# One-core Trainium2 kernel: the order of the last expert rows, of the last gate chunk and of the final stores

## The chip, the cores and the metric

The kernel runs on one core of a Trainium2 chip. The metric is device time in microseconds (us) of one execution; three runs of the kernel before give the median. The profile is of one more execution, and its trace counts from the first instruction of the span.

## What is computed

One layer of a hybrid encoder, 256 tokens by 2048 columns in float32: token mixers, a product-key expert network, and a gated embedding. The change touches the end of it:

```python
def peer_ffn(...):      # 8 heads, 16 experts each, per token
    a = gelu(einsum('thkd,td->thk', expert_u[idx], xb))
    return einsum('thk,thkd->td', g * a, expert_v[idx])
...
h = h + peer_ffn(rmsnorm(h, norm_ffn), ...)
gate = sigmoid(rmsnorm(h, norm_ple) @ w_ple_gate)     # 2048 x 2048
h = h + gate * (p @ w_ple)
return rmsnorm(h, norm_final)
```

## The kernel before

Every engine has its own program, written out by hand, and semaphores order them. Tokens come in two blocks of 128 (b = 0 and 1), one token per partition.

**Experts.** Groups g = 0 to 15 are the eight heads of block 0, then the eight of block 1. For each of the 16 picks of a group GpSimd gathers one row of `peer_u` for each of the 128 tokens into `u_ring` (1 MB, four slots) and one of `peer_v` into `v_ring`. VectorE forms the dot products (L1214). TensorE multiplies each `v_ring` row by a diagonal of weights (`down`, L1657) and adds it up in PSUM: block 0 in `mix`, block 1 in `acc`, each a pair of tiles of 1024 columns. A row is four matmuls of 512 columns, which the trace shows as eight.

**The last group** (g = 15) is shared out. TensorE takes the eight even picks (row j = 0 to 7, `v_ring`), VectorE the eight odd ones (`add_row`, L1305, from `u_ring` straight into `h[:, 1]`). `last_rows` is GpSimd's order of these 16 gathers. TensorE multiplies rows 0 to 5, then slice 0 of the gate product for block 0, then rows 6 and 7, then four matmuls by zero that close the sums (L1705) and release `peer_ready`. Slice 1 for block 0 follows. VectorE adds the two PSUM tiles to `h` (`add_half`, L1259), TensorE transposes block 1 in two items (L1396), VectorE scales them (`t_scale`, L829), ScalarE rounds them to a high part (L538), and VectorE takes the low part (`t_lo_part`, L836).

**The gate product** has four chunks of 512 output columns (ND = 4), and each chunk four slices of 512 rows of the weight (NQ = 4). SyncE loads a slice into `raw` (1 MB), ScalarE rounds it to `wg_hi` (`split_hi`, L547), VectorE forms `wg_lo` (`split_lo`, L846), and TensorE makes 12 matmuls for each block of tokens (`token_slice`, L1414). Three pairs of `wg` buffers rotate, so that `split_hi(s)` waits until slice s - 3 is used (`slice_used`, counted when block 1 of a slice is done). In the middle of the next chunk ScalarE takes the sigmoid (`gate`, L762), and VectorE multiplies it by the embedding, adds it to `h` and forms `hn = h * nrow` (L1346, L1349, L1340).

**After the last chunk** the order is: sigmoid of both blocks on ScalarE (L787), multiply and add on VectorE (L1365, L1367), squares of the last 512 columns on ScalarE (L791), one square root for both blocks (L532), one Newton step on VectorE (`newton`, L810 to L818), then the scaling of `hn`: block 0 on VectorE (L1374), block 1 on ScalarE (L794). SyncE stores each block as one DMA of 1 MB (L397) and waits for both (L332).

Of the kernel before, what the change touches and what calls it, by code (L numbers as in the profile page):

```python
# [22 lines left out]
P = 128  # L23


def build(nc, x, p, norm_mix, w_in, gate_up, gate_bias, gla_norm, conv_w, conv_b, ig_bias, fg_bias,
# [40 lines left out]
    with ctx:  # L67
# [178 lines left out]
        peer_ready, peer_taken = sem("peer_ready"), sem("peer_taken")  # L246
        pt_ready, ple_ready, gate_ready, gate_last = sem("pt_ready"), sem("ple_ready"), sem("gate_ready"), sem("gate_last")
        out_ready = [sem(f"out_ready{b}") for b in range(NB)]
        out_done = sem("out_done")
# [53 lines left out]
        PH_NO = {"A": 0, "B": 1, "G": 2}  # L303
        EARLY = 6
# [27 lines left out]
        with nc.Block() as block:  # L332
# [3 lines left out]
            def _(sp):  # L336
# [58 lines left out]
                for b in range(NB):  # L395
                    sp.wait_ge(out_ready[b], 1)
                    sp.dma_start(out[0, b * P:(b + 1) * P, :], hn[:, b, :]).then_inc(out_done, 16)  # L397
                sp.wait_ge(out_done, 16 * NB)
# [126 lines left out]
            def _(act):  # L525
# [227 lines left out]
                act.wait_ge(peer_ready, NB)  # L753
# [31 lines left out]
                act.wait_ge(slice_used, NQ * (gG + ND))  # L785
                for b in range(NB):
                    act.activation(gt[:, (ND - 1) % 2, b, :], acc_view(gG + ND - 1)[:, b, :], ACT.Sigmoid,  # L787
                                   scale=stat[:, 20 + b:21 + b]).then_inc(gate_last, 1)
                for b in range(NB):
                    act.wait_ge(h_ready, 2 * NB + ND + b)  # L790
                    act.activation(junk_g[b][:, 3 * CW:], h[:, b, 3 * CW:], ACT.Square, accum_out=stat[:, 6 + b:7 + b]).then_inc(ssq_ready, 1)  # L791
                rms_sqrt(4, 6, 8)
                act.wait_ge(rs_ready, 2)
                act.activation(hn[:, 1, :], hn[:, 1, :], ACT.Copy, scale=stat[:, 23:24]).then_inc(out_ready[1], 1)  # L794
# [3 lines left out]
            def _(dve):  # L798
# [457 lines left out]
                def add_half(b, pairs, i):  # L1256
                    dve.wait_ge(peer_ready, b + 1)
                    hv = h[:, b, i * 2 * CW:(i + 1) * 2 * CW]
                    V.tensor_tensor(hv, hv, pairs[i][:, :], ALU.add)  # L1259
                    dve.drain().then_inc(src_ready, 1)  # L1260
# [101 lines left out]
                for b in range(NB):  # L1362
                    dve.wait_ge(gate_last, b + 1)
                    gb = gt[:, (ND - 1) % 2, b, :]
                    V.tensor_tensor(gb, gb, ple_tile(ND - 1)[:, b, :], ALU.mult)  # L1365
                    dve.drain()
                    V.tensor_tensor(h[:, b, cols], h[:, b, cols], gb, ALU.add).then_inc(h_ready, 1)  # L1367
                gain_of(ND - 1)
                dve.wait_ge(ssq_ready, 10)
                V.tensor_tensor(stat[:, 6:8], stat[:, 6:8], stat[:, 24:26], ALU.add)  # L1370
                dve.drain()
                rms_scale(4, 10, 6, 8)
                dve.drain().then_inc(rs_ready, 1)
                V.tensor_scalar(hn[:, 0, :], hn[:, 0, :], stat[:, 22:23], None, ALU.mult).then_inc(out_ready[0], 1)  # L1374
# [3 lines left out]
            def _(pe):  # L1378
# [24 lines left out]
                def token_slice(q, lo_count, blocks=range(NB)):  # L1403
# [5 lines left out]
                    for k in range(KQ):  # L1409
                        kt = q * KQ + k  # L1410
                        for b in blocks:
                            tok = slice(b * P, (b + 1) * P)
                            for n, (a, w) in enumerate(((hi, w_high), (hi, w_low), (lo, w_high))):
                                ins = T.matmul(into[:, b * CW:(b + 1) * CW], a[:, kt, tok], w[:, k, :],  # L1414
                                               start=(kt == 0 and n == 0), stop=(kt == KT - 1 and n == 2))
                    if blocks[-1] == NB - 1:
                        ins.then_inc(slice_used, 1)

# [221 lines left out]
                for b, pairs in enumerate((mix, acc)):  # L1640
# [10 lines left out]
                    def down(g, picks, between=None):  # L1651
                        for k in picks:
# [3 lines left out]
                            for j in range(4):  # L1656
                                ins = T.matmul(pairs[j // 2][:, (j % 2) * CW:(j % 2 + 1) * CW], diag[:, k % DEEP, :],  # L1657
                                               v_ring[:, k % DEEP, j * CW:(j + 1) * CW], start=False, stop=False, skip_group_check=True)
                            ins.then_inc(v_free, 1)
# [17 lines left out]
                    if b == NB - 1:  # L1677
# [21 lines left out]
                        down(G - 1, range(0, 6))  # L1699
                        pe.wait_ge(tlo_done, 10)  # L1700
                        token_slice(0, NQ * gG + 1, blocks=(0,))
                        down(G - 1, range(6, 8))
                    for i in range(2):
                        for j in range(2):
                            ins = T.matmul(pairs[i][:, j * CW:(j + 1) * CW], zero16[:, 0:P], zero16[:, :], start=False, stop=True, skip_group_check=True)  # L1705
                    ins.then_inc(peer_ready, 1)


                token_slice(1, NQ * gG + 2, blocks=(0,))
                transposes("G", (2, 3))  # L1710
# [6 lines left out]
                for c in range(1, ND):  # L1717
                    g = gG + c
                    for q in range(NQ):
                        token_slice(q, g * NQ + q + 1)  # L1720

# [24 lines left out]
```

## Time and profile before

| | us |
|---|---|
| three runs: median (lowest to highest) | 1891.07 (1890.78 to 1891.27) |
| the profiled execution: its own time | 1889.44 |
| the profiled execution: span of its trace | 1887.6 |
| last group: TensorE's row 5 starts | 1766.26 |
| gate matmuls without a break from | 1788.17 |
| last matmul ends | 1872.4 |

TensorE is busy for 1564.6 us (83% of the span), VectorE for 1095.0 (58%), GpSimd for 864.1 (46%), ScalarE for 399.6 (21%). The chain of waits that ended last is, in shares of the span, GpSimd 31%, TensorE 29%, issue 18%, DMA 15%, VectorE 4%. In the expert phase the 16 DMA engines move about 420 GB/s with a busy share of 0.9 or more. In rows of a timeline the columns are start, duration, engine, line, operation, output and input, count, and in brackets the idle time before and what ended it. A busy matmul is modelled and overlaps its neighbour, so the pace is read from starts.

### The profile page before, as it was taken

What the parts mean: (1) busy time and instruction counts of PE and PEld (TensorE: products, weight loads), DVE (VectorE), ACT (ScalarE), POOL (GpSimd) and SP (SyncE); (2) the same over time, 40 slices, a digit from 0 to 9 for tenths busy, and PEclk for the clock granted to TensorE, in tenths of its full rate; (3) what the DMA queues carried; (4) which work ended last, traced back from release to release, by engine and by line L of the source; (5) the groups of instructions that cost most, each with busy time, mean ns of one, the idle gap of its engine ahead of it and who ended that gap; (6) DMA issues with size and microseconds to landing.
All of it is one profiled execution on the core that took longest, in us unless ns stands there. A gap on an engine that the chain in (4) does not pass through costs nothing.

```text
span 1887.6 us, 16206 instructions
## 1 busy us (share of the span) xinstructions
PE 1564.6 (83%) x5380; PEld 917.5 (49%) x5383; DVE 1095.0 (58%) x1519; ACT 399.6 (21%) x558; POOL 864.1 (46%) x1149
## 2 busy tenths in 40 slices
PE   7999999999988987777777777777777777878896
PEld 6998888788844542222222222322222223333485
DVE  4667546554955755556565555655556565554664
ACT  4445445331011110101101011011111101111243
POOL 3000000001675756666666767666666765576200
PEclk9999999999999999999999999999999999999998
DMA  7444545856799999999999999999999999999851
GB/s 229 157 157 158 177 147 168 291 199 256 278 404 421 421 419 419 422 421 422 422 422 422 422 421 421 421 422 422 422 422 422 422 422 421 421 420 416 323 201 67
DMA packets 126353, 648.31 MB, mean 343 GB/s; under 512 B 10076, under 2 KB 10184, under 8 KB 59736
## 3 DMA queue, kind: packets, MB, share of 16 engines
q0 software_dynamic: 74688, 541.59, 69.5%
q1 hardware_dynamic: 51408, 105.91, 16.3%
q8 instruction: 35, 0.57, 0.1%
q14 instruction: 22, 0.18, 0.0%
q10 hardware_dynamic: 200, 0.06, 0.0%
HBM read 645.42 MB, written 2.10 MB: 343 GB/s over the span
## 4 chain that ended last, share of the span: by engine, by line
POOL 31%; PE 29%; issue 18%; DMA 15%; DVE 4%; ACT 1%; DVEq 1%; POOLq 0%; ACTq 0%; SPq 0%
PE acc L1414 16%; DMA v_ring<-in_peer_v_dram,idxv 13%; POOL u_ring L477 9%; POOL v_ring L484 9%; POOL tick L483 9%; PE acc L1427 4%; POOL tick L476 3%; PE acc L1657 3%; PE mix L1414 2%; DMA u_ring<-in_peer_u_dram,idxu 2%; PE mix L1657 1%; DVE u_ring L1214 1%; PE acc L1607 1%; PE mix L1470 1%; POOL tick L447 1%
## 5 line engine op out<-in xcount | busy, mean ns | idle before, releaser
L1214 DVE CUSTOM_DVE_ANT_0 u_ring<-u_ring,xn 128x2048 f32<-128x2048 f32 x256 | 586.6, 2292 | 471.7 <-DMA u_ring<-in_peer_u_dram,idxu 470.3
L1657 PE MATMUL mix<-v_ring,diag 128*128 128x512 f32 x1024 | 479.1, 612 | 145.8 <-DMA v_ring<-in_peer_v_dram,idxv 135.3
L1657 PE MATMUL acc<-v_ring,diag 128*128 128x512 f32 x960 | 442.3, 605 | 138.6 <-DMA v_ring<-in_peer_v_dram,idxv 135.3
L1657 PEld LDWEIGHTS mix<-v_ring,diag 128*128 128x128 f32 x1024 | 188.5, 193 | 420.1 <-issue 249.9
L1657 PEld LDWEIGHTS acc<-v_ring,diag 128*128 128x128 f32 x960 | 174.7, 191 | 403.4 <-issue 224.9
L483 POOL TENSOR_TENSOR tick<-tick 128x1 f32<-128x1 f32 x240 | 212.8, 887 | 322.2 <-PE mix L1657 170.4
L477 POOL DMA_INDIRECT u_ring<-in_peer_u_dram,idxu x256 | 260.9, 1019 | 40.6 <-issue 36.0
L709 ACT ACTIVATE diag<-ident,wgt 128x128 f32<-128x128 f32 x240 | 92.3, 398 | 829.5 <-PE mix L1657 448.5
L484 POOL DMA_INDIRECT v_ring<-in_peer_v_dram,idxv x240 | 243.0, 1013 | 37.7 <-issue 7.0
L846 DVE TENSOR_TENSOR w_lo<-raw,w_hi 128x2048 fp32r<-128x2048 f32 x62 | 142.1, 2292 | 148.5 <-ACT w_hi L547 147.6
L547 ACT ACTIVATE w_hi<-raw 128x2048 fp32r<-128x2048 f32 x64 | 122.5, 1914 | 212.7 <-PE acc L1414 146.9
L1414 PE MATMUL acc<-w_hi,t_hi 128*128 128x512 f32 x384 | 151.4, 394 | 1.8 <-DVE w_lo L846 1.8
L1414 PE MATMUL acc<-w_hi,t_lo 128*128 128x512 f32 x384 | 149.6, 390 | 0.0
L1414 PE MATMUL acc<-w_lo,t_hi 128*128 128x512 f32 x384 | 149.5, 389 | 0.0
L435 POOL DMA_DIRECT2D keys<-in_peer_sub_keys_dram x1 | 1.2, 1201 | 319.3 <-DVE t_lo L836 319.3
L476 POOL TENSOR_TENSOR tick<-tick 128x1 f32<-128x1 f32 x256 | 72.7, 284 | 51.0 <-DVE dots L1214 46.6
L1414 PEld LDWEIGHTS acc<-w_hi,t_hi 128*128 128x128 f32 x384 | 72.1, 188 | 16.5 <-issue 2.2
L1414 PEld LDWEIGHTS acc<-w_hi,t_lo 128*128 128x128 f32 x384 | 72.1, 188 | 15.2
L1414 PEld LDWEIGHTS acc<-w_lo,t_hi 128*128 128x128 f32 x384 | 72.2, 188 | 14.6
L1427 PE MATMUL acc<-t_hi,w_hi 128*128 128x256 f32 x256 | 73.9, 289 | 1.7 <-DVE t_lo L836 1.0
L1427 PE MATMUL acc<-t_hi,w_lo 128*128 128x256 f32 x256 | 73.2, 286 | 0.0
L1427 PE MATMUL acc<-t_lo,w_hi 128*128 128x256 f32 x256 | 73.1, 286 | 0.0
(299 smaller groups left out, 1449.8 us busy)
## 6 DMA issues: line engine op xcount, KB each, us to landing
raw<-in_w_in_dram SPq DMA_DIRECT2D x48, 1024.0 KB, 5.1
raw<-in_w_out_dram SPq DMA_DIRECT2D x16, 1024.0 KB, 5.3
raw<-in_w_ple_gate_dram SPq DMA_DIRECT2D x16, 1024.0 KB, 5.1
raw<-in_peer_query_dram SPq DMA_DIRECT2D x5, 1024.0 KB, 5.1
qw_u<-in_peer_query_dram SPq DMA_DIRECT2D x4, 1024.0 KB, 14.3
qw_v<-in_peer_query_dram SPq DMA_DIRECT2D x4, 1024.0 KB, 9.7
u_ring<-in_peer_u_dram,idxu POOLq DMA_INDIRECT x256, 16.0
v_ring<-in_peer_v_dram,idxv POOLq DMA_INDIRECT x248, 14.9
```

The source lines that it names most:

```text
L447: nc.gpsimd.tensor_tensor(tick[:, c:c + 1], tick[:, c + 4:c + 5], tick[:, c + 4:c + 5], ALU.add)
L476: nc.gpsimd.tensor_tensor(tick[:, 2 * k:2 * k + 1], tick[:, 2 * TOPK + 4:2 * TOPK + 5], tick[:, 2 * TOPK + 5:2 * TOPK + 6], ALU.add)
L477: nc.gpsimd.indirect_dma_start(u_ring[:, k % DEEP, :], None, u_rows, bass.IndirectOffsetOnAxis(idxu[:, e, k:k + 1], 0)).then_inc(u_in[k % ...
L483: nc.gpsimd.tensor_tensor(tick[:, 2 * k + 1:2 * k + 2], tick[:, 2 * TOPK + 4:2 * TOPK + 5], tick[:, 2 * TOPK + 5:2 * TOPK + 6], ALU.add)
L484: nc.gpsimd.indirect_dma_start(v_ring[:, k % DEEP, :], None, v_rows, bass.IndirectOffsetOnAxis(idxv[:, e, k:k + 1], 0)).then_inc(v_in[k % ...
L547: act.activation(high_of(s), raw[:, q, :, :], ACT.Copy).then_inc(hi_done, 1)
L709: act.activation(diag[:, k % DEEP, :], ident[:, :], ACT.Copy, scale=wgt[:, k:k + 1]).then_inc(diag_ready, 1)
L846: V.tensor_tensor(low_of(s), raw[:, q, :, :], high_of(s).bitcast(F32), ALU.subtract).then_inc(lo_done, 1)
L1214: V.tensor_tensor_reduce(out=u_ring[:, k % DEEP, :], in0=u_ring[:, k % DEEP, :], in1=xn2[:, b, :], scale=1.0, scalar=0.0, op0=ALU.mult, op ...
L1414: ins = T.matmul(into[:, b * CW:(b + 1) * CW], a[:, kt, tok], w[:, k, :], start=(kt == 0 and n == 0), stop=(kt == KT - 1 and n == 2))
L1427: ins = T.matmul(acc[set_no][:, c * S:(c + 1) * S], w[:, s_slot, k, c * P:(c + 1) * P], a[:, kt, :], start=(kt == 0 and n == 0 and c % 2 = ...
L1657: ins = T.matmul(pairs[j // 2][:, (j % 2) * CW:(j % 2 + 1) * CW], diag[:, k % DEEP, :], v_ring[:, k % DEEP, j * CW:(j + 1) * CW], start=Fa ...
```

## The change

Six edits, all behind the gather of the last group.

- TensorE multiplies all eight of its last rows one after another. The last row's own matmuls close the sums (`stop`), the zero matmuls stay for block 0 only, and a new semaphore `peer_half` counts after each half of the last row; it replaces `peer_ready` for block 1, and the last row no longer counts in `v_free`.
- Slice 0 of block 0 comes behind the rows, cut in two, with the transposes of block 1 between the halves; slice 1 of block 0 comes behind them.
- In the last chunk slice 0 is multiplied for both blocks, then slices 1 to 3 for block 0 (`gate_first`), then slices 1 to 3 for block 1.
- What follows the last chunk is done per block: sigmoid, multiply, add, squares of the last 512 columns (now on VectorE), square root, Newton step, scaling.
- Each block's scaling is shared: columns 0 to 1279 on VectorE, 1280 to 2047 on ScalarE.
- Each block is stored in two DMAs, in all four.

```diff
@@ -243,9 +243,11 @@
         u_free, v_free = sem("u_free"), sem("v_free")
         top_ready, gelu_ready, w_ready, diag_ready = sem("top_ready"), sem("gelu_ready"), sem("w_ready"), sem("diag_ready")
         exp_ready = sem("exp_ready")
-        peer_ready, peer_taken = sem("peer_ready"), sem("peer_taken")
+        peer_ready, peer_half, peer_taken = sem("peer_ready"), sem("peer_half"), sem("peer_taken")
         pt_ready, ple_ready, gate_ready, gate_last = sem("pt_ready"), sem("ple_ready"), sem("gate_ready"), sem("gate_last")
         out_ready = [sem(f"out_ready{b}") for b in range(NB)]
+        out_rest = [sem(f"out_rest{b}") for b in range(NB)]
+        gate_first = sem("gate_first")
         out_done = sem("out_done")
 
 
@@ -301,6 +303,7 @@
 
         L0 = 11
         PH_NO = {"A": 0, "B": 1, "G": 2}
+        HALF = 1280
         EARLY = 6
 
         def tokens_of(phase):
@@ -393,9 +396,11 @@
                 sp.dma_start(nrow[:, :], norm_final.partition_broadcast(P)).then_inc(nfin_in, 16)
                 stream(w_ple_gate[0], gG + 1, ND - 1, CW)
                 for b in range(NB):
+                    sp.wait_ge(out_rest[b], 1)
+                    sp.dma_start(out[0, b * P:(b + 1) * P, HALF:], hn[:, b, HALF:]).then_inc(out_done, 16)
                     sp.wait_ge(out_ready[b], 1)
-                    sp.dma_start(out[0, b * P:(b + 1) * P, :], hn[:, b, :]).then_inc(out_done, 16)
-                sp.wait_ge(out_done, 16 * NB)
+                    sp.dma_start(out[0, b * P:(b + 1) * P, 0:HALF], hn[:, b, 0:HALF]).then_inc(out_done, 16)
+                sp.wait_ge(out_done, 16 * 2 * NB)
 
 
             @block.gpsimd
@@ -750,7 +755,7 @@
                     act.activation(diag[:, j % DEEP, :], ident[:, :], ACT.Copy, scale=wgt[:, k:k + 1]).then_inc(diag_ready, 1)
                 act.wait_ge(v_free, DEEP + (G - 1) * TOPK + 6)
                 split_hi(NQ * gG + 1)
-                act.wait_ge(peer_ready, NB)
+                act.wait_ge(peer_half, 2)
                 t_hi_part("G", (2, 3))
                 split_hi(NQ * gG + 2)
 
@@ -782,16 +787,16 @@
                 act.wait_ge(h_ready, 2 * NB + ND - 1)
                 for b in range(NB):
                     act.activation(junk_g[b][:, 0:3 * CW], h[:, b, 0:3 * CW], ACT.Square, accum_out=stat[:, 24 + b:25 + b]).then_inc(ssq_ready, 1)
-                act.wait_ge(slice_used, NQ * (gG + ND))
                 for b in range(NB):
+                    if b == 0:
+                        act.wait_ge(gate_first, 1)
+                    else:
+                        act.wait_ge(slice_used, NQ * (gG + ND))
                     act.activation(gt[:, (ND - 1) % 2, b, :], acc_view(gG + ND - 1)[:, b, :], ACT.Sigmoid,
                                    scale=stat[:, 20 + b:21 + b]).then_inc(gate_last, 1)
-                for b in range(NB):
-                    act.wait_ge(h_ready, 2 * NB + ND + b)
-                    act.activation(junk_g[b][:, 3 * CW:], h[:, b, 3 * CW:], ACT.Square, accum_out=stat[:, 6 + b:7 + b]).then_inc(ssq_ready, 1)
-                rms_sqrt(4, 6, 8)
-                act.wait_ge(rs_ready, 2)
-                act.activation(hn[:, 1, :], hn[:, 1, :], ACT.Copy, scale=stat[:, 23:24]).then_inc(out_ready[1], 1)
+                    rms_sqrt(4 + b, 6 + b, 7 + b)
+                    act.wait_ge(rs_ready, 2 + b)
+                    act.activation(hn[:, b, HALF:], hn[:, b, HALF:], ACT.Copy, scale=stat[:, 22 + b:23 + b]).then_inc(out_rest[b], 1)
 
 
             @block.vector
@@ -1254,7 +1259,10 @@
 
 
                 def add_half(b, pairs, i):
-                    dve.wait_ge(peer_ready, b + 1)
+                    if b == 0:
+                        dve.wait_ge(peer_ready, 1)
+                    else:
+                        dve.wait_ge(peer_half, i + 1)
                     hv = h[:, b, i * 2 * CW:(i + 1) * 2 * CW]
                     V.tensor_tensor(hv, hv, pairs[i][:, :], ALU.add)
                     dve.drain().then_inc(src_ready, 1)
@@ -1364,14 +1372,21 @@
                     gb = gt[:, (ND - 1) % 2, b, :]
                     V.tensor_tensor(gb, gb, ple_tile(ND - 1)[:, b, :], ALU.mult)
                     dve.drain()
-                    V.tensor_tensor(h[:, b, cols], h[:, b, cols], gb, ALU.add).then_inc(h_ready, 1)
-                gain_of(ND - 1)
-                dve.wait_ge(ssq_ready, 10)
-                V.tensor_tensor(stat[:, 6:8], stat[:, 6:8], stat[:, 24:26], ALU.add)
-                dve.drain()
-                rms_scale(4, 10, 6, 8)
-                dve.drain().then_inc(rs_ready, 1)
-                V.tensor_scalar(hn[:, 0, :], hn[:, 0, :], stat[:, 22:23], None, ALU.mult).then_inc(out_ready[0], 1)
+                    V.tensor_tensor(h[:, b, cols], h[:, b, cols], gb, ALU.add)
+                    dve.drain()
+                    dve.wait_ge(ssq_ready, 8)
+                    V.tensor_tensor_reduce(out=junk_g[b][:, cols], in0=h[:, b, cols], in1=h[:, b, cols], scale=1.0, scalar=0.0,
+                                           op0=ALU.mult, op1=ALU.add, accum_out=stat[:, 6 + b:7 + b])
+                    dve.drain()
+                    V.tensor_tensor(stat[:, 6 + b:7 + b], stat[:, 6 + b:7 + b], stat[:, 24 + b:25 + b], ALU.add)
+                    dve.drain()
+                    v, r, w = stat[:, 14 + b:15 + b], stat[:, 22 + b:23 + b], nwt[:, 0:1]
+                    V.tensor_scalar(v, stat[:, 6 + b:7 + b], 1.0 / D, EPS, ALU.mult, ALU.add).then_inc(var_ready, 1)
+                    V.tensor_tensor(hn[:, b, cols], h[:, b, cols], nrow[:, cols], ALU.mult)
+                    dve.wait_ge(sqrt_ready, 4 + b)
+                    newton(r, v, w)
+                    dve.drain().then_inc(rs_ready, 1)
+                    V.tensor_scalar(hn[:, b, 0:HALF], hn[:, b, 0:HALF], r, None, ALU.mult).then_inc(out_ready[b], 1)
 
 
             @block.tensor
@@ -1400,13 +1415,13 @@
                     if uses is not None:
                         pe.wait_ge(acc_free[set_no], uses)
 
-                def token_slice(q, lo_count, blocks=range(NB)):
+                def token_slice(q, lo_count, blocks=range(NB), ks=range(KQ)):
 
                     hi, lo = tokens_of("G" if lo_count > NQ * gG else "B")
                     w_high, w_low = high_of(lo_count - 1), low_of(lo_count - 1)
                     into = acc_of((lo_count - 1) // NQ)
                     pe.wait_ge(lo_done, lo_count)
-                    for k in range(KQ):
+                    for k in ks:
                         kt = q * KQ + k
                         for b in blocks:
                             tok = slice(b * P, (b + 1) * P)
@@ -1415,6 +1430,7 @@
                                                start=(kt == 0 and n == 0), stop=(kt == KT - 1 and n == 2))
                     if blocks[-1] == NB - 1:
                         ins.then_inc(slice_used, 1)
+                    return ins
 
                 def column_slice(q, lo_count):
 
@@ -1648,15 +1664,18 @@
                         for j in range(2):
                             T.matmul(pairs[i][:, j * CW:(j + 1) * CW], zero16[:, 0:P], zero16[:, :], start=True, stop=False, skip_group_check=True)
 
-                    def down(g, picks, between=None):
+                    def down(g, picks, between=None, last=None):
                         for k in picks:
 
                             pe.wait_ge(diag_ready, g * TOPK + k + 1)
                             pe.wait_ge(v_in[k % DEEP], 16 * (TOPK // DEEP) * g + 16 * (k // DEEP + 1))
                             for j in range(4):
                                 ins = T.matmul(pairs[j // 2][:, (j % 2) * CW:(j % 2 + 1) * CW], diag[:, k % DEEP, :],
-                                               v_ring[:, k % DEEP, j * CW:(j + 1) * CW], start=False, stop=False, skip_group_check=True)
-                            ins.then_inc(v_free, 1)
+                                               v_ring[:, k % DEEP, j * CW:(j + 1) * CW], start=False, stop=(k == last), skip_group_check=True)
+                                if k == last and j % 2 == 1:
+                                    ins.then_inc(peer_half, 1)
+                            if k != last:
+                                ins.then_inc(v_free, 1)
                             if between is not None:
                                 between(k)
 
@@ -1696,28 +1715,36 @@
 
                         down(G - 2, range(TOPK))
                         transposes("G", (0, 1))
-                        down(G - 1, range(0, 6))
-                        pe.wait_ge(tlo_done, 10)
-                        token_slice(0, NQ * gG + 1, blocks=(0,))
-                        down(G - 1, range(6, 8))
-                    for i in range(2):
-                        for j in range(2):
-                            ins = T.matmul(pairs[i][:, j * CW:(j + 1) * CW], zero16[:, 0:P], zero16[:, :], start=False, stop=True, skip_group_check=True)
-                    ins.then_inc(peer_ready, 1)
-
-
+                        down(G - 1, range(len(pe_picks)), last=len(pe_picks) - 1)
+                    if b == 0:
+                        for i in range(2):
+                            for j in range(2):
+                                ins = T.matmul(pairs[i][:, j * CW:(j + 1) * CW], zero16[:, 0:P], zero16[:, :], start=False, stop=True, skip_group_check=True)
+                        ins.then_inc(peer_ready, 1)
+
+
+                pe.wait_ge(tlo_done, 10)
+                token_slice(0, NQ * gG + 1, blocks=(0,), ks=range(0, KQ // 2))
+                transposes("G", (2, 3))
+                token_slice(0, NQ * gG + 1, blocks=(0,), ks=range(KQ // 2, KQ))
                 token_slice(1, NQ * gG + 2, blocks=(0,))
-                transposes("G", (2, 3))
                 pe.wait_ge(tlo_done, 11)
                 for q in range(2):
                     token_slice(q, NQ * gG + q + 1, blocks=(1,))
                 pe.wait_ge(tlo_done, 12)
                 for q in range(2, NQ):
                     token_slice(q, NQ * gG + q + 1)
-                for c in range(1, ND):
+                for c in range(1, ND - 1):
                     g = gG + c
                     for q in range(NQ):
                         token_slice(q, g * NQ + q + 1)
+                g = gG + ND - 1
+                token_slice(0, g * NQ + 1)
+                for q in range(1, NQ):
+                    ins = token_slice(q, g * NQ + q + 1, blocks=(0,))
+                ins.then_inc(gate_first, 1)
+                for q in range(1, NQ):
+                    token_slice(q, g * NQ + q + 1, blocks=(1,))
 
 
 # ---- launch: one core; inputs and outputs as the reference has them ----
```

## Rows read from the trace of the kernel before

**Rows 1.** The chain of waits in order of time: start us, us, what it was.

```profile
1766.26 3.67 PE acc L1657 x8
1769.93 2.79 PE mix L1414 x12
1772.72 6.87 PE acc L1657 x16
...
1783.20 0.89 PE acc L1396 x8
...
1788.17 40.14 PE mix L1414 x168
1828.31 44.07 PE acc L1414 x192
...
1872.40 0.70 ACT gt L787
```

**Rows 2.** Busy time by stretches: us, engines, granted clock (PEclk), DMA share, GB/s.

```profile
1760.00:1765.00 5.00, 3.67 (x8) 1.44 (x8) 2.38 (x2) 0.40 (x1) 3.14 (x4) 1.00 1.02 424
...
1788.10:1791.00 2.90, 2.83 (x7) 2.25 (x8) 2.43 (x3) 2.90 (x2) 0.00 (x0) 0.50 0.00 0
```

**Rows 3.** The timeline, TensorE, at the gap ahead of block 1's slices.

```profile
1788.17 0.80 PE L1414 MATMUL mix<-wg_hi,t_hi_gate 128*128 128x512 f32 x1 [3.23 <-DVE t_lo_gate L836]
...
1789.19 0.63 PE L1414 MATMUL mix<-wg_hi,t_lo_gate 128*128 128x512 f32 x1
1789.62 0.63 PE L1414 MATMUL mix<-wg_hi,t_hi_gate 128*128 128x512 f32 x1
```

**Rows 4.** The timeline, VectorE, from the last added row on.

```profile
1774.12 2.34 DVE L1305 SCALAR_TENSOR_TENSOR h<-u_ring,wgt,h 128x2048 f32<-128x2048 f32 x1
1780.49 2.56 DVE L1259 TENSOR_TENSOR h<-h,acc 128x1024 f32<-128x1024 f32 x2 [4.02 <-PE acc L1705]
1784.11 1.22 DVE L829 TENSOR_TENSOR tfp_gate<-acc,par 128x1024 f32<-128x1024 f32 x1 [1.06 <-PE acc L1396]
...
1786.89 2.36 DVE L836 TENSOR_TENSOR t_lo_gate<-tfp_gate,t_hi_gate 128x1024 fp32r<-128x1024 f32 x2
```

**Rows 5.** One tile's DMAs (raw slices from 1765 us, then the two stores): us to landing.

```profile
DMA to landing us min/median/max: 4.9/5.1/12.4
...
DMA to landing us min/median/max: 3.9/4.8/5.7
```

**Rows 6.** The timeline, VectorE: the last slice's low part.

```profile
1859.70 2.28 DVE L846 TENSOR_TENSOR wg_lo<-raw,wg_hi 128x2048 fp32r<-128x2048 f32 x1
```

**Rows 7.** The timelines, VectorE and ScalarE, behind the last matmul.

```profile
1873.12 0.69 DVE L1365 TENSOR_TENSOR gt<-gt,ple 128x512 f32<-128x512 f32 x1 [11.14 <-ACT gt L787]
1873.88 0.69 DVE L1367 TENSOR_TENSOR h<-h,gt 128x512 f32<-128x512 f32 x1
...
1878.25 0.17 DVE L810 RECIPROCAL stat<-stat 128x2 f32<-128x2 f32 x1 [0.67 <-ACT stat L532]
...
1879.53 1.29 DVE L1374 TENSOR_SCALAR u_ring<-u_ring,stat 128x2048 f32<-128x2048 f32 x1 [0.17 <-issue]
...
1876.71 1.28 ACT L532 ACT_TABLE_LOAD   x1
1878.01 0.20 ACT L532 ACTIVATE stat<-stat 128x2 f32<-128x2 f32 x1
1879.47 2.00 ACT L794 ACTIVATE u_ring<-u_ring,stat 128x2048 f32<-128x2048 f32 x1 [1.26 <-DVEq L1373]
```

**Rows 8.** The page's costliest groups: one sum over 2048 columns.

```profile
L1214 DVE CUSTOM_DVE_ANT_0 u_ring<-u_ring,xn 128x2048 f32<-128x2048 f32 x256 | 586.6, 2292 | 471.7 <-DMA u_ring<-in_peer_u_dram,idxu 470.3
```

**Rows 9.** The timeline, ScalarE: table loads at one wait and at two.

```profile
1637.71 1.28 ACT L702 ACT_TABLE_LOAD   x1
1653.21 0.21 ACT L702 ACTIVATE act_a<-dots 128x16 f32<-128x16 f32 x1 [14.21 <-DVE dots L1214]
...
1806.41 1.28 ACT L762 ACT_TABLE_LOAD   x1 [3.67 <-PE mix L1414]
```

## The prediction

> **What bounds the kernel now.** The page comes first: up to about 1770 us the 16 DMA engines run at 0.9 or more of their time, so the gathers set the pace there, and the change touches none of them. Next I read the chain of waits behind the last gathers. It is short: TensorE's row 5, slice 0 of block 0, rows 6 and 7, the zero matmuls and slice 1, transposes, VectorE's scaling and low parts; then 360 gate matmuls from 1788.17 to 1872.4, and a serial tail from there to the end of the span at 1887.6 [rows 1]. The stretches show the clock: 1.00 of full speed (2.4 GHz) in the row phase in spite of TensorE's short pauses, and 0.50 (1.2 GHz) for 2.9 us after the pause of 3.23 us at 1788.17 [rows 2, 3]. The timelines of VectorE and ScalarE then give what each step waits for. So three stretches count: rows to 1788.17, the last chunk, and the tail.
>
> **Part 1, rows first, slices behind them.** Now row 5 is followed by 12 matmuls (2.79 us) although rows 6 and 7 are next in the chain; then 6.87 us for two rows, 3.44 each [rows 1]. All gathers were issued before this, so their landings don't move. A row is 1 MB, 2.5 us at 420 GB/s: TensorE waited for row 5 until 1766.26, so row 6 is due at 1768.6 and row 7 at 1771.1, both ahead of their turn. New times on the old clock:
> - Rows: row 6 starts at 1766.26 + 3.44 = 1769.7, row 7 at 1773.1 and ends at 1776.6; its first half is done at 1774.9.
> - VectorE: its last `add_row` runs 1774.12 to 1776.5 as before [rows 4]. The half sums are 2.56 / 2 = 1.28 each, so 1777.8 and 1779.1. They started at 1780.49, after 4.02 us of waiting [rows 4]. `add_row` is now what they wait for, not TensorE.
> - TensorE: 6 matmuls (2.79 / 2 = 1.4) to 1778.0; 8 transposes (0.89, say 0.95) to 1779.0; the second item waits for the second half sum, 1779.2 to 1780.1; 1.4 to 1781.5; slice 1, 2.8, to 1784.3. If `add_row` came later, everything behind the transposes would come as much later.
> - VectorE: the first scaling follows the half sums at once, 1779.2, since its transposes are done (before, it waited 1.06 for them). From the first scaling to the gate's restart took 1788.17 - 1784.11 = 4.06 [rows 3, 4], which gives 1783.3.
> TensorE is the later, so block 1's slices start at 1784.3, not 1788.17: **3.9 us earlier**. The same matmuls remain. The zero matmuls (0.8) fall away inside that number.
>
> The pause of 3.23 us is gone as well; the longest left is about 0.2. The first 168 matmuls took 40.14, where the next 192 ran at 44.07 / 192 = 0.2295 each [rows 1], so they lost 40.14 - 38.6 = 1.6; the slow ones alone are six at 0.43 [rows 3], six times 0.2, so 1.2. I take **1.4 us** back. The ends for this part: 3.9 (nothing back) and 5.5. I take 5.3. The Trainium skill (TensorE: Matmul & The Clock Gate, What's actually happening) says that the number of slow matmuls at a warm-up differs from run to run; the row here is one draw, and by that rule a given run of the kernel before may lose less than 1.4 there, down to nothing, and the sum below would then be -7.9 and not -9.3.
>
> Can the slices be fed 5 us earlier? SyncE loads raw slices 2 and 3 when row 7 lands, which stays. Their landing took at most 12.4 us [rows 5], which for slice 2 would be 1783.5; ScalarE's turn for it comes at 1783.1, behind two roundings. Then 1.9 + 2.3 gives 1787.5, and TensorE wants it at 1784.3 + 5.5 = 1789.8. Later slices are paced by TensorE's own use of them. Cost nothing; cover 2.3 us.
>
> **Part 2, the last chunk by blocks.** Count from the end of chunk 2, call it C (before: 1872.4 - 96 x 0.2295 = 1850.3). The buffer of slice 3 is free when slice 0 is used by both blocks, C + 5.5, which is before VectorE gets to it. VectorE's last `split_lo` started at 1859.70 and ended at 1861.98 = C + 11.65; ahead of it stand the sigmoid that waits for C, slice 2's split and three elementwise steps [rows 6]. Before, TensorE wanted slice 3 at C + 72 x 0.2295 = C + 16.5. Now it wants it after slice 0 for two blocks and slices 1 and 2 for one: 48 x 0.2295 = C + 11.0. **A new wait of 0.6 us** (0.3 to 1.0) on `split_lo(3)`, which moves the last matmul from C + 22.05 to C + 22.7. It is paid in full. Block 0 is ready at C + 11.65 + 12 x 0.23 + 0.2 = C + 14.6, some 8 us ahead of block 1. All that belongs to block 0 (6.2 us, below) is hidden under block 1's matmuls and ends at C + 20.8, its two stores at about C + 26.
>
> **Part 3, the tail of block 1.** E is the last matmul. Before: sigmoid 0.7 each, two multiplies and adds for two blocks, squares, a table load of 1.28 exposed between the squares and the root, root, Newton, then 2.00 on ScalarE: E + 9.1, the end at 1881.5 [rows 7]. Now: sigmoid 0.7 [rows 1] (E + 0.72); multiply and add, 0.76 from start to start, to E + 2.2; squares of 512 columns as one VectorE instruction with accumulation, which the trace has only at 2048 columns, 2.29 [rows 8]; the subtraction of a slice takes 2.28 at that size and a 512-column product 0.69 [rows 6, 7], so 0.69 and some 0.1 to read the sum out; two small steps of 0.2, to E + 3.45. Its bounds are 0.69 and 2.29, and the equal pace at 2048 decides for the lower. The root's table load starts behind the sigmoid and ends at E + 2.0: hidden. Root 0.2, beside it `hn` 0.69, to E + 4.1; Newton 1.2 (1878.25 to 1879.53, with a gap of 0.1 at its end [rows 7]), E + 5.3. Scaling 1280 columns on VectorE: 1.29 for 2048, 0.22 of it fixed by my estimate, so 0.9; 768 on ScalarE, between 0.70 for 512 and 2.00 for 2048, also 0.9 [rows 1, 7]. Both at **E + 6.2, against 9.1**.
>
> One instruction is easy to miss: ScalarE needs the sigmoid table again for block 1. It can start at C + 20.8 and ends at C + 22.1, 0.6 ahead of E. That holds if the load goes ahead of the wait for TensorE. With one wait ahead of the instruction it does (load at 1637.71, instruction at 1653.21), with two it came behind (1806.41, idle for TensorE) [rows 9]. Here there is one. So nothing; 1.3 if I am wrong. The Trainium skill (ScalarE: Activation LUTs, What ACT_TABLE_LOAD costs) gives 2.66 us for a switch, load and drain. The trace shows the root 0.02 behind a load of 1.28 [rows 7]; by the page the load would end 0.7 after E, and the sum would be 0.7 smaller.
>
> **Stores.** Before, 2 MB start at 1880.85; landings took 3.9 and 5.7 [rows 5], the second from 1881.5 to 1887.2, the span ends at 1887.6. Now 1 MB is left behind E: issued at E + 6.2 and 6.6. By the first store (3.9 for 1 MB with an empty queue) it ends at E + 10.1, plus 0.4 to the span's end; by a raw load (5.1) at E + 11.7. Stores in rows of 3 and 5 KB are not in the trace; I take E + 10.6, nearer the store. **Before E + 15.2: 4.6 us less**, from 3.5 to 4.8.
>
> **Sum.** -5.3 + 0.6 - 4.6 = -9.3 us against the profiled 1889.44. The median is 1.6 above that execution; the same difference there gives 1891.07 - 9.3 = 1881.8.
>
> **Rivals.**
> - Small losses in the tail (17%): the table load behind the wait (+1.3) and stores at the raw load's 5.1 (+1.1): 1884.2. For it: no row has a single wait at that sigmoid or a short store. Against: the pair of rows on loads.
> - The front gains nothing (11%): block 1's slices start early, but the feed (raw loads at 12.4, two roundings, the squares on ScalarE ahead of slice 3) is late by what was won, or `add_row`'s gather is: 1881.8 + 5.3 = 1887.1. Against: 2.3 us of cover, and `add_row` at 1774.12 was not waiting.
> - Slower (3%): the new wait of 0.6 in the last chunk drops the clock to half, and the 48 matmuls left take 0.43 instead of 0.23: +9.6, 1891.4. It decides from the 47th slow matmul on. Against: in the row phase TensorE pauses for 1.3 us in each 5.00 (3.67 busy) at 1.00 [rows 2].
> - The forecast, with its own spread of 1880.3 to 1883.3: 69%.
>
> **How the numbers follow.** Within 0.2% (3.8 us) a measurement can't tell from no change. The range runs from the sum of all upper ends (5.5, 0.3, 4.8: 1881.1, less 1 for what I see too large, as the pauses or the Newton step) to between the two rivals: 1880.0 to 1885.8. Faster by over 0.2% means under 1887.3: 0.90, with part of the second rival; within 0.2%: 0.08; slower: 0.02, as the third rival must exceed its own sum.
>
> **What would show it.** Row 7 ending near 1776.6; half sums at 1776.6 straight behind `add_row`; no TensorE pause over 0.3 to the last chunk and no 0.50 stretch; block 1's slices at 1784.3; one pause of 0.6 on `wg_lo` in the last chunk; a sigmoid table load ending before the last matmul; 6.2 from there to the last scaling and 4.4 more to the end. Wrong if `add_row` waits for its gather, if the wait on `wg_lo` exceeds 1, or if the last store takes over 5.

## The result, and the profile after

The changed kernel takes 1879.03 us (median of six runs, 1877.94 to 1883.05) against 1890.92 for six runs of the kernel before. The ratio is 0.9947 with a 95% interval of 0.9932 to 0.9962, so 10.0 us less (7.2 to 12.9). The forecast was 9.3 less, and a range of 1880.0 to 1885.8. By the ratio the time is 0.9947 x 1891.07 = 1881.0; the median of the six runs itself lies 1.0 under the range.

Runs of this kernel scatter by more than was visible at first: the start of TensorE's row 5 lies between 1763.8 and 1770.1 us in the thirteen profiles of this study, whatever the kernel, and no edit acts ahead of it. So all comparisons of traces below count from the first matmul of row 5 to the end of the span, **R** for short. Before, R is 1887.6 - 1766.26 = 121.3; after, 1876.3 - 1763.94 = 112.4: 9.0 less.

TensorE's timeline after, at the rows (the answer to the first lines of [rows 1] and to [rows 3]); columns are start, duration, engine, line, operation, count, idle before:

```profile
1763.94 10.54 PE L1673 MATMUL acc<-v_ring,diag 128*128 128x512 f32 x24 [1.30 <-DMA v_ring<-in_peer_v_dram,idxv]
1773.91 0.80 PE L1429 MATMUL mix<-wg_hi,t_hi_gate 128*128 128x512 f32 x1
...
1775.71 2.26 PE L1411 MATMUL acc<-ident,h 128*128 128x128 f32 x16
1777.73 0.48 PE L1429 MATMUL mix<-wg_hi,t_hi_gate 128*128 128x512 f32 x1
...
1781.94 0.40 PE L1429 MATMUL mix<-wg_hi,t_hi_gate 128*128 128x512 f32 x1
```

Three rows in one piece, six matmuls, 16 transposes, the rest of slice 0 and slice 1. The row at 1781.94 is the nineteenth matmul from 1777.73 and the first of block 1: 18.0 behind row 5, where it was 21.9 before. None of these rows has idle time ahead of it but the first.

VectorE's timeline after (against [rows 4]):

```profile
1771.80 2.34 DVE L1313 SCALAR_TENSOR_TENSOR h<-u_ring,wgt,h 128x2048 f32<-128x2048 f32 x1
1774.23 2.56 DVE L1267 TENSOR_TENSOR h<-h,acc 128x1024 f32<-128x1024 f32 x2
1777.14 1.23 DVE L834 TENSOR_TENSOR tfp_gate<-acc,par 128x1024 f32<-128x1024 f32 x1 [0.34 <-PE acc L1411]
```

The half sums follow the last added row at once; the 4.02 us of waiting for TensorE are gone.

Then the chain of waits (start, us, what), from the rows to the last chunk:

```profile
1763.94 3.69 PE acc L1673 x8
1767.64 1.92 ACT wg_hi L552
1769.59 2.29 DVE wg_lo L851
1771.88 2.26 DVEq L1315
...
1776.88 1.09 PE acc L1411 x8
1777.97 42.69 PE mix L1429 x186
1820.66 21.96 PE acc L1429 x96
...
1852.06 2.29 DVE wg_lo L851
1854.35 0.04 issue
1854.40 11.34 PE acc L1429 x48
1865.76 0.70 ACT gt L795
```

The chain leaves TensorE behind row 5 and goes over a slice's split and the last added row on VectorE; rows 6 and 7 are no longer on it. What is left between row 5 and the half sums is this split, which stands ahead of the added row in VectorE's order; no run moved it. The 186 matmuls run at 42.69 / 186 = 0.2295 each: nothing is slow. The last 168 of them take 1820.66 - 1781.94 = 38.7, where they took 40.14 before. The chain leaves TensorE again in the last chunk, for `split_lo(3)`. The timeline of TensorE at that place:

```profile
1853.29 0.39 PE L1429 MATMUL acc<-wg_hi,t_lo_gate 128*128 128x512 f32 x1
...
1854.40 0.50 PE L1429 MATMUL acc<-wg_hi,t_hi_gate 128*128 128x512 f32 x1 [0.72 <-DVE wg_lo L851]
...
1854.73 0.40 PE L1429 MATMUL acc<-wg_lo,t_hi_gate 128*128 128x512 f32 x1
```

At the pace of 0.23 the matmul at 1854.40 would have started at 1853.52, so it is 0.88 late, and the next start is 0.33 behind it and not 0.23: 1.0 us in all, more than the 0.72 that the row calls idle, because that counts from the modelled end of the matmul before. The granted clock stays at 1.00; a view of busy time by stretches (PEclk is third from the end):

```profile
1853.30:1854.40 1.10, 0.38 (x3) 0.01 (x1) 1.04 (x1) 0.60 (x2) 0.00 (x0) 1.00 0.00 0
1854.40:1865.80 11.40, 11.33 (x48) 8.93 (x48) 4.59 (x13) 4.44 (x6) 0.00 (x0) 1.00 0.12 49
```

The tail, against [rows 7] and [rows 9], ScalarE's timeline:

```profile
1857.50 0.69 ACT L795 ACTIVATE gt<-acc,stat 128x512 f32<-128x512 f32 x1 [3.60 <-PE acc L1429]
...
1862.67 0.94 ACT L799 ACTIVATE u_ring<-u_ring,stat 128x768 f32<-128x768 f32 x1 [1.48 <-DVEq L1388]
1863.63 1.28 ACT L795 ACT_TABLE_LOAD   x1
1865.76 0.69 ACT L795 ACTIVATE gt<-acc,stat 128x512 f32<-128x512 f32 x1 [0.85 <-PE acc L1429]
1866.47 1.28 ACT L537 ACT_TABLE_LOAD   x1
```

Block 0's sigmoid starts at 1857.50 under block 1's matmuls. The load of the sigmoid table for block 1 goes ahead of the wait for TensorE and ends at 1864.91, 0.83 before the last matmul. VectorE's and SyncE's last rows:

```profile
1868.06 0.69 DVE L1378 CUSTOM_DVE_ANT_0 u_ring<-h 128x512 f32<-128x512 f32 x1
...
1870.99 0.89 DVE L1389 TENSOR_SCALAR u_ring<-u_ring,stat 128x1280 f32<-128x1280 f32 x1 [0.17 <-issue]
...
1871.90 0.33 SPq L400 DMA_DIRECT2D out_dram<-u_ring  x1
1872.28 0.43 SPq L402 DMA_DIRECT2D out_dram<-u_ring  x1
```

Both scalings are done at 1871.88, 6.1 behind the last matmul at 1865.74, and the span ends 10.6 behind it.

### The profile page after: what moved, and what is told of

Same layout as the page of the kernel before. It is cut to its first block, busy times and chain, and to the rows that moved or that the text cites. A ratio compares the mean times of both kernels' runs of the same rounds, so it can differ in the third digit from the quotient of the medians.

```text
span 1876.3 us, 16224 instructions
## 1 busy us (share of the span) xinstructions
PE 1562.2 (83%) x5377; PEld 914.6 (49%) x5379; DVE 1098.2 (59%) x1532; ACT 401.0 (21%) x558; POOL 860.6 (46%) x1149
## 4 chain that ended last, share of the span: by engine, by line
POOL 31%; PE 29%; issue 18%; DMA 15%; DVE 4%; ACT 1%; DVEq 1%; POOLq 0%; ACTq 0%; SPq 0%
PE acc L1429 15%; DMA v_ring<-in_peer_v_dram,idxv 13%; POOL u_ring L482 9%; POOL v_ring L489 9%; POOL tick L488 9%; PE acc L1443 4%; POOL tick L481 3%; PE mix L1429 2%; PE acc L1673 2%; DMA u_ring<-in_peer_u_dram,idxu 2%; DVE u_ring L1219 1%; PE mix L1673 1%; PE acc L1623 1%; PE mix L1486 1%; POOL tick L452 1%
```

## The experiments

Eleven more runs were made, of seven new kernels and four repeats (e1, e9, e10, e11), each with five or more timed executions beside the kernel before on the same chip. R is from the profile. e1 to e4 shared one chip, e5 to e8 a second, e9 to e11 a third.

| run | what | R, us | ratio to before (95%) |
|---|---|---|---|
| before | | 121.3 | |
| after | the change | 112.4 | 0.9947 (0.9932 to 0.9962) |
| e1_again | the change | 112.4 | 0.9949 (0.9936 to 0.9963) |
| e2_front | part 1 alone | 116.0 | 0.9973 (0.9962 to 0.9984) |
| e3_tail | parts 2 and 3 alone | 118.9 | 0.9977 (0.9968 to 0.9986) |
| e4_oldorder | last chunk's slices as before | 118.7 | 0.9982 (0.9973 to 0.9991) |
| e5_onestore | one store per block | 112.3 | 0.9953 (0.9939 to 0.9967) |
| e6_nowait | last low part first | 111.9 | 0.9958 (0.9945 to 0.9972) |
| e7_best | and block 1's squares later | 111.3 | 0.9944 (0.9930 to 0.9958) |
| e8_warm | before, pause filled with matmuls | 120.0 | 0.9995 (0.9986 to 1.0004) |
| e9_before | before, unedited | 120.1 | 1.0004 (0.9995 to 1.0013) |
| e10_after | the change | 112.3 | 0.9959 (0.9946 to 0.9972) |
| e11_best | as e7 | 111.3 | 0.9947 (0.9935 to 0.9960) |

**e1_again**, the change once more.

> The changed kernel once more, as the base for the parts sent with it. I measure each kernel from the first matmul of TensorE's row 5 (of the last group) to the end of the span: 121.3 us before, 112.4 after, a difference of 9.0. Theory 1 (my sum is right, the rest of the measured gain is scatter of what comes ahead of the change): 112.4 again, the start of row 5 scatters by some us from run to run in both kernels, and the median is 9 to 10 us under the one of before. Theory 2 (the change also moves something ahead of row 5): row 5 starts at 1764 here and at 1766 in every kernel whose expert rows are as before, and the difference of the medians is 11 to 12.

R is 1877.8 - 1765.44 = 112.4. Row 5 started at 1765.44 here, at 1763.94 in the first profile of the same kernel, and at 1763.78 in e3_tail, whose expert rows are those of before. Theory 2 falls: the start of row 5 does not follow the kernel.

**e2_front**, part 1 alone: the functions behind the last chunk are those of before.

```diff
-                for c in range(1, ND - 1):
+                for c in range(1, ND):
                     g = gG + c
                     for q in range(NQ):
                         token_slice(q, g * NQ + q + 1)
-                g = gG + ND - 1
-                token_slice(0, g * NQ + 1)
...
```

> Part 1 alone: rows 5 to 7 one after another, slices of block 0 and transposes behind them; last chunk, tail and stores as before. Theory 1: 3.9 us from the earlier restart and 1.1 from the clock that doesn't fall, so 116.3 from row 5 to the end, 5.0 under before; no stretch at a granted clock of 0.50 ahead of the last matmul. Rival (the front is hidden, since the feed of slices is late by what was won): under 2 us.

R is 1880.8 - 1764.76 = 116.0, 5.3 under the first profile of before and 4.1 under e9_before, whose clock did not fall; the timed runs give 5.1 (3.0 to 7.2). The chain has the same 186 matmuls in 42.71 as the change. The rival (under 2) falls: the slices keep up.

**e3_tail**, the other half: rows, slices of block 0 and transposes in the order of before, the rest changed.

```diff
-                        down(G - 1, range(len(pe_picks)), last=len(pe_picks) - 1)
+                        down(G - 1, range(0, 6))
+                        pe.wait_ge(tlo_done, 10)
+                        token_slice(0, NQ * gG + 1, blocks=(0,))
+                        down(G - 1, range(6, 8))
...
```

> Last chunk by blocks, tail by block and four stores alone; rows and transposes as before. Theory 1: wait of 0.7 on the last low part, tail shorter by 4.6, so 117.3 from row 5 to the end, 4.0 under before, and the two parts add up to the whole (5.0 + 4.0). Rival (the parts overlap in effect, as the clock's state at the last chunk depends on the gap ahead): the sum of the two parts misses 9.0 by over 1 us.

R is 1882.7 - 1763.78 = 118.9, only 2.4 under before, and the two parts add up to 7.7 and not 9.0. By the letter of the expectation that is the rival. But the 1.3 us lie behind the pause, not at the last chunk. The chain of e3_tail:

```profile
1785.69 41.48 PE mix L1426 x168
1827.17 21.96 PE acc L1426 x96
...
1860.91 11.32 PE acc L1426 x48
```

The same 168 matmuls took 40.14 in [rows 1], and 38.80 in e8_warm and e9_before below, where the clock stays at 1.00. The stretches of e3_tail show why:

```profile
1783.00:1786.00 3.00, 0.30 (x1) 0.31 (x2) 2.81 (x3) 2.70 (x3) 0.00 (x0) 0.78 0.21 75
1786.00:1789.00 3.00, 3.00 (x8) 2.32 (x8) 2.52 (x2) 3.00 (x3) 0.00 (x0) 0.50 0.00 0
1789.00:1792.00 3.00, 3.00 (x10) 2.32 (x9) 0.54 (x1) 2.73 (x5) 0.00 (x0) 0.58 0.34 60
```

Half clock for some 6 us instead of 3, behind the same pause: against the 38.80, 2.7 us lost instead of 1.3. With that taken out the tail is worth 2.4 + 1.3 = 3.7, near the 4.0 expected. The timed runs, which hold many draws of this, give 5.1 + 4.3 = 9.4 for the parts and 9.6 for the whole (e1_again) on one chip, each with some 2 us either way. e8 and e9 follow this up.

**e4_oldorder**, the whole change but for the order of slices in the last chunk.

```diff
-                token_slice(0, g * NQ + 1)
-                for q in range(1, NQ):
-                    ins = token_slice(q, g * NQ + q + 1, blocks=(0,))
-                ins.then_inc(gate_first, 1)
-                for q in range(1, NQ):
-                    token_slice(q, g * NQ + q + 1, blocks=(1,))
+                for q in range(NQ):
+                    token_slice(q, g * NQ + q + 1)
```

> The whole change, but slices 1 to 3 of the last chunk are multiplied for both blocks as before. Theory 1: no wait on the last low part (0.7 gained), but block 0's 6.2 us of tail now stand ahead of block 1's, with a sigmoid table load of 1.3 between them: the end comes 18.0 us behind the last matmul and not 10.6, so 119.2 from row 5 to the end, 6.8 over the change. Rival (the gain of the tail is the move of the squares, the split scaling and the smaller stores, and not the order of the slices): within 2 us of the change.

R is 1884.3 - 1765.63 = 118.7, 6.3 over the change. The two sigmoids in its chain of waits, with the table load ahead of the second:

```profile
1866.45 0.70 ACT gt L791
...
1872.58 1.28 ACT L791
1873.87 0.70 ACT gt L791
```

Block 1's tail stands 7.4 behind block 0's, and the end comes 17.9 behind the last matmul. A tail by blocks without slices by blocks throws away more than the tail gains: R is even 2.7 over that of e2_front, which has the tail of before. So the order of the slices is what makes part 3 pay, and the rival falls. The order with the tail of before was not run.

**e5_onestore**, two stores instead of four.

```diff
-                    sp.dma_start(out[0, b * P:(b + 1) * P, HALF:], hn[:, b, HALF:]).then_inc(out_done, 16)
                     sp.wait_ge(out_ready[b], 1)
-                    sp.dma_start(out[0, b * P:(b + 1) * P, 0:HALF], hn[:, b, 0:HALF]).then_inc(out_done, 16)
-                sp.wait_ge(out_done, 16 * 2 * NB)
+                    sp.dma_start(out[0, b * P:(b + 1) * P, :], hn[:, b, :]).then_inc(out_done, 16)
+                sp.wait_ge(out_done, 16 * NB)
```

> The whole change, but each block is stored as one DMA of 1 MB once both of its parts are scaled. Theory 1 (what shortens the stores is that only 1 MB is left behind the last matmul, not the parts): the store starts 6.2 us behind the last matmul, takes 3.9 as the first store of before did, and the end comes 10.5 behind it, against 10.6: 112.3 from row 5 to the end, no difference. Rival (the parts matter, as the first can move while the second is issued): 0.4 to 1.0 later.

R is 1882.4 - 1770.14 = 112.3. One tile's DMAs, first in e5_onestore (two of 1 MB), then in the change (four):

```profile
DMA to landing us min/median/max: 3.9/3.9/3.9
```

```profile
DMA to landing us min/median/max: 2.4/3.0/3.6
```

In [rows 5] the two stores took 3.9 and 5.7, the second while the first was in flight. So from the last scaling to the end of the span it is 4.4 us now, 6.1 before, because block 0's store is out of the way. The four parts give nothing over two.

**e6_nowait**, VectorE's order in the last chunk.

```diff
-                        if q == 2 and g > gG:
+                        if q == (3 if g == gG + ND - 1 else 2) and g > gG:
                             add_ple(g - gG - 1)
                             gain_of(g - gG - 1)
```

> The whole change, and VectorE takes the last slice's low part ahead of chunk 2's three elementwise steps. Theory 1: TensorE's wait of 0.7 in the last chunk is gone, but the squares of 1536 columns on ScalarE now end 15.3 us behind chunk 2 and block 0's sigmoid waits for them, so that block 1's sigmoid table load ends about 0.7 behind the last matmul: 0.3 less in all, 112.1 from row 5 to the end. Rival: the wait was all there was to it, 0.7 less.

R is 1878.5 - 1766.60 = 111.9, 0.5 under the change where 0.3 was expected. TensorE no longer waits, but ScalarE ends its squares at 1860.7 and the load of the sigmoid table at 1868.04, where block 1's sigmoid then starts (1868.05). By R alone the gain lies midway between 0.3 and the rival's 0.7; the trace decides, as the sigmoid starts 0.6 behind the last matmul (1867.42), held by the load. The rival (0.7 without a price) falls.

**e7_best**, and ScalarE's squares of block 1 behind block 0's sigmoid.

```diff
-                for b in range(NB):
-                    act.activation(junk_g[b][:, 0:3 * CW], h[:, b, 0:3 * CW], ACT.Square, accum_out=stat[:, 24 + b:25 + b]).then_inc(ssq_ready, 1)
+                def squares(b):
+                    act.activation(junk_g[b][:, 0:3 * CW], h[:, b, 0:3 * CW], ACT.Square, accum_out=stat[:, 24 + b:25 + b]).then_inc(ssq_ready, 1)
+
+                squares(0)
...
                                    scale=stat[:, 20 + b:21 + b]).then_inc(gate_last, 1)
+                    if b == 0:
+                        squares(1)
...
-                    dve.wait_ge(ssq_ready, 8)
+                    dve.wait_ge(ssq_ready, 7 + b)
```

> As the one before, and ScalarE takes block 1's squares of 1536 columns behind block 0's sigmoid. Theory 1: block 0's sigmoid starts 14.0 behind chunk 2, the table load ends 0.6 ahead of the last matmul, and both the wait of 0.7 and the load are hidden: 111.5 from row 5 to the end, 0.9 under the change. Rival: block 0's root now waits for the squares of block 1 and the table load behind them, and nothing is won over the change.

R is 1878.9 - 1767.61 = 111.3. ScalarE's timeline of e7_best:

```profile
1860.20 0.69 ACT L797 ACTIVATE gt<-acc,stat 128x512 f32<-128x512 f32 x1
1860.79 1.48 ACT L789 ACTIVATE u_ring<-h 128x1536 f32<-128x1536 f32 x1
1862.17 0.19 ACT L789 ACTIVATION_READ_ACCUMULATOR u_ring<-h 128x1 f32 x1
1862.37 1.28 ACT L537 ACT_TABLE_LOAD   x1
1863.70 0.20 ACT L537 ACTIVATE stat<-stat 128x1 f32<-128x1 f32 x1
```

Squares and load fit between the sigmoid and VectorE's step for the root, and the chain of waits has the last 192 matmuls in one piece of 44.10. The last matmul ends 100.8 behind row 5, 101.8 in the change. These 1.0 us are what the wait on the low part cost; R falls by 1.1.

**e8_warm**, the kernel before with its pause filled.

```diff
                 transposes("G", (2, 3))
+                for _ in range(13):
+                    T.matmul(mix[1][:, 0:CW], zero16[:, 0:P], zero16[:, :], start=True, stop=True, skip_group_check=True)
                 pe.wait_ge(tlo_done, 11)
```

> The kernel before, with 13 matmuls of zeros (128x512, bf16) into an unused PSUM tile in TensorE's pause of 3.2 us behind the transposes of block 1; what is computed stays the same. Theory 1 (the pause costs clock beside its own length): no stretch at 0.50 behind it, the 168 gate matmuls of the first two chunks take 38.7 us and not 40.1 or 41.5, and the time from row 5 to the end falls by 1.5 to 2.9. Rival (the clock falls for some other reason, or zeros don't keep it up): 0.50 stays and so does the time.

Block 1's slices start 1789.47 - 1767.56 = 21.9 behind row 5, as before. The chain of e8_warm and its stretch there:

```profile
1789.47 38.80 PE mix L1414 x168
```

```profile
1789.00:1792.00 3.00, 2.58 (x12) 2.09 (x12) 2.52 (x3) 3.00 (x3) 0.00 (x0) 1.00 0.00 0
```

The clock stays at 1.00, and R is 1887.6 - 1767.56 = 120.0, 1.3 less than the first profile of before. The timed runs give 0.9 less with an interval from 2.6 less to 0.8 more: a gain of this size and none can't be told apart there.

**e9_before**, the kernel before without an edit.

> The kernel before once more, unedited, for a second draw of the clock and of the start of row 5. Theory 1 (the length of the slow stretch behind the pause of 3.2 us differs from run to run): the 168 matmuls behind it take between 39.5 and 42 us, 1 to 3 over the 38.7 without the pause, with a granted clock of 0.50 in part of it; all else from row 5 to the end is the same to 0.1. Rival (1.6 us is a fixed cost, and the 2.9 of the run with the new tail came from the edit): 40.1 again.

This was a miss for both. The chain and the stretches of e9_before:

```profile
1788.84 38.80 PE mix L1414 x168
1827.64 44.07 PE acc L1414 x192
```

```profile
1785.00:1788.00 3.00, 0.61 (x6) 0.37 (x4) 2.67 (x3) 1.55 (x2) 0.00 (x0) 1.00 0.59 216
1788.00:1791.00 3.00, 2.16 (x9) 1.80 (x10) 2.52 (x3) 3.00 (x3) 0.00 (x0) 1.00 0.00 0
```

The pause is there and the clock did not fall at all: 38.80, as with the pause filled. R is 1887.0 - 1766.93 = 120.1. So behind the same pause three profiles lost 0, 1.3 and 2.7 us. It also takes back what e8_warm seemed to show: R and the 38.80 are the same without the zeros, so that they kept the clock up is not shown.

**e10_after** and **e11_best**, the pair again on one chip.

> The changed kernel a third time, as the pair of the last one here: 112.4 from row 5 to the end, 9 to 10 us under before in time.

> The change with the last low part ahead of chunk 2's elementwise steps and block 1's squares behind block 0's sigmoid, again: 111.3 from row 5 to the end, 1.1 under the change in every profile; in the timed runs some 0.5 to 1.5 under the change, which their scatter of about 2 us may hide.

R is 1877.4 - 1765.13 = 112.3 and 1875.6 - 1764.30 = 111.3. The medians are 1880.76 and 1878.31, against 1888.47 for before. e11_best is the faster by 2.4 us of the medians, and its five timed executions (up to 1878.96) all lie under the five of e10_after (from 1879.25), but the intervals of the ratios to before overlap. e1 and e7, 0.9 apart, ran on different chips. The size of 1.0 us is shown by the traces (R is 112.3 to 112.4 in three profiles of the change and 111.3 in both of this version), and not by the timed runs. With this the version that beats both kernels is e7's.

## Why the prediction was right, and where not

The sum was right as a whole and in most of its terms. Counted from row 5:

| term | forecast | profile |
|---|---|---|
| block 1's slices start earlier | -3.9 | -3.9 (21.9 to 18.0) |
| clock given back (168 matmuls) | -1.4 | -1.4 here (40.14 to 38.72); near 0 to -2.7 by run |
| wait on `split_lo(3)` | +0.6 | +1.0 |
| last matmul to the end of the span | -4.6 (15.2 to 10.6) | -4.6 (15.2 to 10.6) |
| sum | -9.3 | -9.0 by R (the rounded terms give -8.9) |

- **Rows and half sums.** Row 7 was to end 10.3 behind row 5 and the half sums to start there, behind `add_row`: the measured values are 10.5 and 1774.23 - 1763.94 = 10.3. The feed of slices held; e2_front shows the part alone at -5.3.
- **The clock.** The weak step is "I take 1.4 us back". It was met in this pair, and by luck: it makes one profile's slow stretch a term of the sum. e9_before shows the same pause without any loss, and e3_tail a loss of 2.7. The prediction did name the ends for this, 3.9 and 5.5 for part 1, and a sum of -7.9 if nothing comes back; against e9_before the change is worth 120.1 - 112.3 = 7.8 us, against the first profile 9.0. Its 1.6 is 0.2 too high, since 40.14 runs from a start to the end of the last matmul, and 38.6 counts starts alone (38.72 when measured the same way). What the profiles show is the direction: the clock fell in two of three with the empty pause, and in none of the nine with the new front (1.00 throughout, 186 matmuls in 42.69 to 42.71 each). The mean of the loss is open, as three draws don't give it. By the Trainium skill (TensorE: Matmul & The Clock Gate, What's actually happening) the number of slow matmuls at a warm-up differs from run to run; the traces agree, with 0, 1.3 and 2.7 us lost.
- **The new wait.** It is where it was said to be and was mis-sized: 1.0, the upper end that was named, and not 0.6. The prediction counted TensorE's wish from the end of chunk 2's last matmul, but the next chunk's first matmul starts 0.2 before that end, the low part ended 0.1 later than counted, and the restart costs another 0.1. e7_best removes it and gives back 1.0.
- **The tail.** 6.1 from the last matmul to the scalings, 6.2 forecast; the squares on VectorE took 0.69, the lower bound. How the 3.0 us that this is shorter than before divide was not run apart; by the rows, the root's table load of 1.28 no longer stands in the way and the last scaling takes 0.9 instead of 2.00. The table load came ahead of the wait, as with the single wait in [rows 9], and ended 0.83 before it was needed (0.6 forecast). The 2.66 us for a switch that the Trainium skill (ScalarE: Activation LUTs, What ACT_TABLE_LOAD costs) gives are not borne out: the load at 1863.63 would then have held the sigmoid until 1866.29, and it started at 1865.76. In e7_best the root starts 0.05 behind the end of its load.
- **The stores.** The term is right and so is its reason: 1 MB left behind the last matmul. The four parts, which the change brings, are worth nothing (e5_onestore). Without the order of the slices the split of the tail loses (e4_oldorder).
- **The level.** The median of the first three runs, 1891.07, was high for this kernel; later sets of 12 to 23 runs gave 1888.5 to 1889.2. The ratios of the change in three sets, 0.9947, 0.9949 and 0.9959, mean 7.7 to 10.0 us.
- **The rivals.** Small losses in the tail, no gain in front and a clock that falls behind the 0.7 us wait: none of them happened; the clock was 1.00 behind the wait.

## What to carry to other kernels

When a product of two halves is followed by a serial tail, finish one half's product early: the tail of that half and its store then cost nothing, and here a tail by halves paid only with that order. Check in the same breath who prepares the operands that are now wanted sooner, and put that step ahead of work that nobody waits for. Count such margins from start to start of the matmuls, not from a modelled end. And compare traces from a common event just ahead of the change, where the runs scatter ahead of it by more than the change is worth.

## What the runs showed of the hardware

With the same pause of TensorE (3.2 us) the clock stayed at 1.00 in one profile of the kernel before, and fell to half for about 3 us of matmuls in another and 6 us in e3_tail, whose code is the same up to there. In those two it fell inside the pause: it was 1.00 at its start and 0.50 when the matmuls began again. Pauses of 1.3 us in each 5 us kept it at 1.00 in the six profiles whose row phase was read. It stayed at 1.00 too with thirteen bf16 matmuls of zeros in the pause, in the one profile taken, which shows no effect of theirs, as it did so once without them.

A store of 1 MB landed in 3.9 us with no other in flight, and in 5.7 us as the second of two. The load of ScalarE's sigmoid table (1.28 us) ran ahead of the single wait for TensorE, from 1863.63 where the sigmoid started at 1865.76.
